# A hybrid mixer and mixture-of-experts layer on one core: read-back, the last block's rows and the final norm arranged otherwise

## What is computed

```python
h = h + moe_ffn(rms_norm(h, norm_ffn_w))       # 4 of 32 experts for each token
out = rms_norm(h, norm_final_w)[:, N_META:]

def run_block(tok, g, e):                      # one block of tokens of one expert
    gu = xt[tok] @ w_gate_up[e] + b_gate_up[e]
    act = glu * sigmoid(1.702 * glu) * (lin + 1.0)
    return (act @ w_down[e] + b_down[e]) * g[:, None]
```

## Time and profile before

| | |
|---|---|
| median of 3 runs | 1552.45 us (1552.38 to 1553.67) |
| the profiled execution | 1552.11 us, span 1550.5 us |
| TensorE busy | 98% of the span |
| VectorE, ScalarE, GpSimd busy | 39%, 16%, 21% |
| mean granted clock of TensorE | 0.993 |
| bytes moved | 476.68 MB, mean 307 GB/s |

### The profile page before, as it was taken

The page is one execution under the profiler, slowest core; times in us unless marked ns, Lnnn a source line. Parts: engine busy times, 40 slices in busy tenths (PEclk is TensorE's granted clock), DMA queues, the critical chain, the costliest instruction groups (busy, mean ns, idle before and its releaser), DMA issues.

```text
span 1550.5 us, 38142 instructions
## 1 busy us (share of the span) xinstructions
PE 1513.8 (98%) x15427; PEld 1005.0 (65%) x15427; DVE 612.0 (39%) x1251; ACT 254.1 (16%) x343; POOL 326.2 (21%) x509
## 2 busy tenths in 40 slices
PE   9999999999999999999999999999999999999996
PEld 7998899877863556555656665655567565565552
DVE  6768988878254132211222112321123211232125
ACT  4533434256130000000000000000000000000011
POOL 1000000000033323322233222332222322233320
PEclk9999999999999999999999999999999999999997
DMA  4222222431368999999999999999999999999937
GB/s 150 83 98 107 89 89 108 162 136 55 136 238 294 416 418 416 406 408 412 410 408 399 400 409 408 403 405 395 414 404 406 403 405 417 410 413 401 368 121 277
DMA packets 80357, 476.68 MB, mean 307 GB/s; under 512 B 17318, under 2 KB 17966, under 8 KB 26434
## 3 DMA queue, kind: packets, MB, share of 16 engines
q1 hardware_dynamic: 66066, 459.14, 73.8%
q0 software_dynamic: 14256, 17.05, 3.1%
HBM read 467.54 MB, written 17.01 MB: 313 GB/s over the span
## 4 chain that ended last, share of the span: by engine, by line
PE 93%; DVE 4%; issue 1%; ACT 1%; DMA 0%; POOLq 0%; DVEq 0%; POOL 0%; ACTq 0%; SPq 0%
PE bank L1768 66%; PE bank L1450 15%; PE bank L1642 6%; PE bank L1469 1%; DVE w_lo L944 1%; PE bank L1578 1%; PE bank L1581 0%; PE bank L1709 0%; PE bank L1593 0%; PE bank L1579 0%; PE bank L1608 0%; DVE reg_tq L1034 0%; PE bank L1837 0%; DVE reg_tq L960 0%; PE bank L1705 0%
## 5 line engine op out<-in xcount | busy, mean ns | idle before, releaser
L1768 PE MATMUL bank<-ring,moe_f 128*32 128x512 f32 (+1 forms) x12216 | 1018.6, 485 | 11.5 <-DVE moe_f L1398 1.1
L1768 PEld LDWEIGHTS bank<-ring,moe_f 128*32 128x32 f32 x12216 | 598.9, 110 | 430.4 <-issue 351.7
L1380 DVE STREAM_TRANSPOSE moe_f<-bank 128x768 f32<-128x768 f32 x32 | 31.5, 983 | 610.2 <-PE bank L1768 610.2
L609 POOL DMA_INDIRECT moe_f<-n_scratch,idx_next x96 | 100.1, 1043 | 438.7 <-DVE moe_f L1364 415.0
L1450 PE MATMUL bank<-n_hi,w_hi 128*128 128x258 f32 (+2 forms) x608 | 190.7, 314 | 1.8 <-DVE w_lo L944 1.8
L1450 PE MATMUL bank<-n_lo,w_hi 128*128 128x258 f32 (+2 forms) x608 | 186.4, 307 | 0.0
L1450 PE MATMUL bank<-n_hi,w_lo 128*128 128x258 f32 (+2 forms) x608 | 186.2, 306 | 0.0
L892 ACT ACTIVATE moe_f<-moe_f 128x768 f32<-128x768 f32 x32 | 27.1, 846 | 717.2 <-DVE moe_f L1384 716.2
L1450 PEld LDWEIGHTS bank<-n_hi,w_hi 128*128 128x128 f32 x608 | 114.4, 188 | 9.7 <-DVE w_lo L944 2.2
L616 POOL DMA_INDIRECT expert_rows<-moe_f,idx_now x96 | 98.3, 1024 | 104.2 <-ACT moe_f L898 82.7
L1450 PEld LDWEIGHTS bank<-n_lo,w_hi 128*128 128x128 f32 x608 | 114.5, 188 | 6.9 <-issue 1.7
(11 more groups left out here) (280 smaller groups left out, 1014.6 us busy)
## 6 DMA issues: line engine op xcount, KB each, us to landing
ring<-in_moe SPq DMA_DIRECT2D x381, 1024.0 KB, 7.9
ring<-in_w_in SPq DMA_DIRECT2D x24, 1024.0 KB, 4.9
ring<-in_w_out SPq DMA_DIRECT2D x8, 1024.0 KB, 4.8
ring<-expert_rows SPq DMA_DIRECT2D x8, 1024.0 KB, 12.2
ring<-acs_scratch SPq DMA_DIRECT2D x4, 1024.0 KB, 7.1
idx_raw<-slot_table POOLq DMA_DIRECT2D x140, 0.8 KB
reg_vcs<-in_xT SPq DMA_DIRECT2D x4, 528.0 KB, 6.1
reg_x<-in_xrow SPq DMA_DIRECT2D x4, 512.0 KB, 4.9
```

What stands on the lines that cost most here:

```text
L609: g.indirect_dma_start(out=xg[:, n, :], out_offset=None, in_=n2_parts, in_offset=bass.IndirectOffsetOnAxis(ap=idx_next[:, 2 * n:2 * n + 1] ...
L1380: v.transpose(glu.rearrange("p b (g r) -> p g b r", g=GRANULES), gate).then_inc(gate_raw, 1)
L1768: ins = mm(out[l * LANE:(l + 1) * LANE, g * width:(g + 1) * width], x[:, at, g * LANE:(g + 1) * LANE], w[:, l * width:(l + 1) * width], st ...
```

## The change

- SyncE waits for the scatters of all blocks but the last before it reads the rows back, and each of the eight loads goes to a ring place of its own among `slot(4)` to `slot(11)`. The count of blocks less one is worked out and stored beside the count.
- The last block's rows are not scattered. `expert_rows` is filled with zeros early on (GpSimd clears `reg_k` and issues eight DMAs of 1 MB between tiles of the mixer), so that its places read as zero. ScalarE and VectorE copy the last block's y out of PSUM to `y_last` [96 slots, 1024], and TensorE adds it to each tile through a matrix `last_of` [96 slots, 512 tokens] that holds the gate where slot and token belong together. VectorE forms `last_of` from the slots' token numbers, from token numbers that GpSimd writes (`tok_iota`), and from a row of the last expert's gates that TensorE spreads over 96 partitions after block 0's down product (four products of 128 columns, from `last_gate`).
- The bias products leave the tail: blocks 2 to 5 are written out on TensorE, and behind each `down(j - 1)` come the two products of one tile, to PSUM banks 3 and 7. VectorE adds them to h2 in the same block.
- In the final norm, the multiply by the reciprocal root and that by the weight are done by GpSimd for tiles 0 to 2, as two instructions. Tile 3 stays with VectorE.

```diff
+        zero_parts = yk_d.rearrange("(n p r) d -> n p (r d)", n=KC, p=P)
...
-        def yk(m):
-            return view(ring, m * TOPK * D, TOPK, D) if m < 3 else view(ring2, 0, TOPK, D)
-
+        def y_of(l, n):
+            at = n * QUARTER
+            return bank[l * LANE:(l + 1) * LANE, 4 + at // 512, at % 512:at % 512 + QUARTER]
+
+        def yk(m, hf):
+            return slot(GU - DN + 2 * m + hf).rearrange("p (k d) -> p k d", k=2)
+
+        y_last = view(moe_f, 3584, D)
+        last_gate = view(late_a, 6336, TT, P)
+        tok_iota = view(late_a, 7456, SEQ)
+        last_of = view(moe_f, 8448, SEQ)
...
-        PART_BANK = [6, 0, 2, 4]
+        PART_BANK = [0, 2, 6, 4]
...
-            hold(y_out, n_blocks * (16 * GRANULES))
+            ahead = sp.value_load(blocks[0:1, 2 * LIST + 5:2 * LIST + 6], min_val=EXPERTS - 1, max_val=LIST - 2)
+            hold(y_out, ahead * (16 * GRANULES))
             for m in range(TT):
                 rows = yk_d.rearrange("(k t) d -> t k d", k=TOPK)[m * P:(m + 1) * P]
                 for hf in range(2):
-                    sp.dma_start(yk(m)[:, 2 * hf:2 * hf + 2, :], rows[:, 2 * hf:2 * hf + 2, :]).then_inc(yk_in[hf][m], 16)
+                    sp.dma_start(yk(m, hf), rows[:, 2 * hf:2 * hf + 2, :]).then_inc(yk_in[hf][m], 16)
             for m in range(TT):
-                sp.wait_ge(o_ready, m + 1)
+                if m < TT - 1:
+                    sp.wait_ge(o_ready, m + 1)
+                else:
+                    sp.wait_ge(o_last, 1)
                 sp.dma_start(out_d[m * P:(m + 1) * P, :], o_sb[m]).then_inc(out_out, 16)
...
+            steps.done(g.memset(reg_k[:, :], 0.0))
...
+            for n in range(KC):
+                pool.wait_ge(xbc_ready, n + 2)
+                pool.dma_start(zero_parts[n], reg_k[:, :]).then_inc(table_filled, 16)
             pool.wait_ge(xbc_ready, XBC_TILES)
+            pool.wait_ge(table_filled, 16 * (1 + KC))
...
+            pool.wait_ge(first_done, 2)
+            for q in range(GRANULES):
+                g.iota(tok_iota[q * LANE:(q + 1) * LANE, :], pattern=[[LANES, SEQ]], base=q, channel_multiplier=0,
+                       allow_small_or_imprecise_dtypes=True).then_inc(slot_iota_ready, 1)
+            pool.wait_ge(slot_iota_ready, 2 + GRANULES)
...
-            hold((y_ready, n_blocks + 1))
-            scatter()
-
+            for m in range(TT - 1):
+                pool.wait_ge(o_scale, m + 1)
+                steps.done(g.tensor_scalar(o_sb[m], o_sb[m], small[:, m:m + 1], None, ALU.mult))
+                steps.settled()
+                g.tensor_tensor(o_sb[m], o_sb[m], w_fin, ALU.mult).then_inc(o_ready, 1)
...
-            evict(n_blocks - 1)
+            act.wait_ge(dn_used, n_blocks * DN + 2 * DN)
+            for l in range(2):
+                for n in range(GRANULES):
+                    ins = a.copy(y_last[n * LANE:(n + 1) * LANE, l * QUARTER:(l + 1) * QUARTER], y_of(l, n))
+            ins.then_inc(y_ready, 1)
...
-            with dve.Fori(1, n_blocks) as j:
-                activations(j, dve.value_load(blocks[0:1, ds(2 * j + 1, 1)], min_val=0, max_val=EXPERTS - 1))
+            last = dve.value_load(blocks[0:1, ds((n_blocks - 1) * 2 + 1, 1)], min_val=0, max_val=EXPERTS - 1)
+            steps.settled()
+            for m in range(TT):
+                v.tensor_scalar(last_gate[:, m, :], ident[:, :], gm[:, m, ds(last, 1)], None, ALU.mult).then_inc(diag_ready, 1)
+
+            def expert_of(j):
+                return dve.value_load(blocks[0:1, ds(2 * j + 1, 1)], min_val=0, max_val=EXPERTS - 1)
+
+            activations(1, 1)
+            with dve.Fori(2, 2 + TT) as j:
+                activations(j, expert_of(j))
+                dve.wait_ge(bias_done, j)
+                row = h2[:, ds(j - 2, 1), :].rearrange("p o (h d) -> p (o h) d", h=2)
+                for hf in range(2):
+                    ins = v.tensor_tensor(row[:, hf, :], row[:, hf, :], bank[:, 3 + 4 * hf, :], ALU.add)
+                ins.then_inc(h2_ready, 1)
+            with dve.Fori(2 + TT, n_blocks) as j:
+                activations(j, expert_of(j))
...
+            dve.wait_ge(idx_moved, n_blocks * 4 + 1)
+            for n in range(GRANULES):
+                p = slice(n * LANE, (n + 1) * LANE)
+                steps.done(v.tensor_copy(pos_f[p, 0:1], idx_now[p, 2 * n:2 * n + 1]))
+            steps.settled()
+            dve.wait_ge(slot_iota_ready, 2 + GRANULES)
+            dve.wait_ge(bias_done, 1)
+            v.scalar_tensor_tensor(last_of[0:BLOCK, :], tok_iota[0:BLOCK, :], pos_f[0:BLOCK, 0:1], bank[0:BLOCK, 6, :],
+                                   ALU.is_equal, ALU.mult).then_inc(diag_ready, 1)
+            dve.wait_ge(dn_used, n_blocks * DN + 2 * DN)
+            for l in range(2, LANES):
+                for n in range(GRANULES):
+                    ins = v.tensor_copy(y_last[n * LANE:(n + 1) * LANE, l * QUARTER:(l + 1) * QUARTER], y_of(l, n))
+            ins.then_inc(diag_ready, 1)
+            dve.wait_ge(h2_ready, 2 * TT)
...
+                if m < TT - 1:
+                    v.reciprocal(small[:, m:m + 1], small[:, m:m + 1]).then_inc(o_scale, 1)
+                    continue
                 steps.done(v.reciprocal(small[:, m:m + 1], small[:, m:m + 1]))
                 steps.settled()
                 v.scalar_tensor_tensor(o_sb[m], o_sb[m], small[:, m:m + 1], w_fin, ALU.mult, ALU.mult
-                                       ).then_inc(o_ready, 1)
+                                       ).then_inc(o_last, 1)
...
-            with pe.Fori(2, n_blocks) as j:
+            pe.wait_ge(diag_ready, TT)
+            for m in range(TT):
+                ins = mm(bank[0:BLOCK, 6, m * P:(m + 1) * P], ones[:, 0:BLOCK], last_gate[:, m, :], start=m == 0, stop=m == TT - 1,
+                         skip_group_check=True)
+            ins.then_inc(bias_done, 1)
+            pe.wait_ge(gmT_ready, 1)
+            pe.wait_ge(bd_in, 16)
+            for j in range(2, 2 + TT):
+                gate_up(j)
+                down(j - 1)
+                pe.wait_ge(h2_ready, j + (TT - 2))
+                for hf in range(2):
+                    ins = mm(bank[:, 3 + 4 * hf, :], gT[0:EXPERTS, j - 2, :], b_down[0:EXPERTS, hf * 512:(hf + 1) * 512], start=True, stop=True)
+                ins.then_inc(bias_done, 1)
+            with pe.Fori(2 + TT, n_blocks) as j:
                 gate_up(j)
                 down(j - 1)
             down(n_blocks - 1, GU)
 
-            pe.wait_ge(gmT_ready, 1)
-            pe.wait_ge(bd_in, 16)
+            pe.wait_ge(diag_ready, 3 * TT + 1)
             for m in range(TT):
-                b = PART_BANK[m]
                 if m == TT - 1:
                     pe.wait_ge(y_ready, n_blocks + 1)
-                for hf in range(2):
-                    mm(bank[:, b + hf, :], gT[0:EXPERTS, m, :], b_down[0:EXPERTS, hf * 512:(hf + 1) * 512],
-                       start=True, stop=False)
-            pe.wait_ge(diag_ready, 2 * TT)
-            for m in range(TT):
+                    pe.wait_ge(diag_ready, 3 * TT + 2)
                 pe.wait_ge(yk_in[0][m], 16)
                 for k in range(2):
                     for hf in range(2):
-                        ins = mm(bank[:, PART_BANK[m] + hf, :], diag[:, 2 * m + k, :], yk(m)[:, k, hf * 512:(hf + 1) * 512],
-                                 start=False, stop=k == 1)
+                        mm(bank[:, PART_BANK[m] + hf, :], diag[:, 2 * m + k, :], yk(m, 0)[:, k, hf * 512:(hf + 1) * 512],
+                           start=k == 0, stop=False)
+                pe.wait_ge(y_ready, n_blocks + 1)
+                pe.wait_ge(diag_ready, 3 * TT + 2)
+                for hf in range(2):
+                    ins = mm(bank[:, PART_BANK[m] + hf, :], last_of[0:BLOCK, m * P:(m + 1) * P], y_last[0:BLOCK, hf * 512:(hf + 1) * 512],
+                             start=False, stop=True)
                 ins.then_inc(part_done, 1)
```

More of the change, by code:

```diff
@@ L311, in build @@
         staged, conv_ready, xbc_ready = sem("staged"), sem("conv_ready"), sem("xbc_ready")
-        dt_done, dt_raw, dt_e = sem("dt_done"), sem("dt_raw"), sem("dt_e")
+        dt_done, dt_e = sem("dt_done"), sem("dt_e")
         acs_ready, wend_e, pk_ready, dtk_done, dtk_ready = (
@@ L332, in build @@
         first_kept, first_turned, stack_ready, xT_half = [sem("first_kept0"), sem("first_kept1")], sem("first_turned"), sem("stack_ready"), sem("xT_half")
[L333 to L334 removed]
+        n2T_done, n2T_ready, logit_done, top_ready, gate_e = (
+            sem("n2T_done"), sem("n2T_ready"), sem("logit_done"), sem("top_ready"), sem("gate_e"))
         rank_done, pos_ready, table_out, list_ready, list_out, list_in = (
@@ L348, in build @@
         diag_ready, part_done = sem("diag_ready"), sem("part_done")
+        o_scale, o_last = sem("o_scale"), sem("o_last")
         sp_passed, pool_passed = sem("sp_passed"), sem("pool_passed")
@@ L1022, in _ @@
```

(7 more changed lines are left out.)

5 lines of the change are left out of this document (1 added, 4 removed).

## The result

The changed kernel took 1557.40 us (median of 7 runs, 1556.43 to 1560.97), the kernel before 1552.45 (7 runs, 1551.75 to 1553.67). The ratio is 1.0033, with a 95% interval of 1.0023 to 1.0043: slower, by more than the 0.2% that can be told. The forecast was 1546.3, its range ended at 1552.5. The profiled execution took 1558.03 us, its span is 1556.4.

The account below looks back on a forecast made before the run. TensorE sets the pace in the experts' blocks, then a chain of waits the tail: 1552.1 - 13.1 + 6.8 + 1.0 - 2.4 - 0.2 + 1.6 + 0.2 = 1546.0, with the median's 0.3 1546.3 us; range 1542.5 to 1552.5.

Parts of the forecast that it names:

- Norm and weight of tiles 0 to 2 on GpSimd: Tail: VectorE's last norm may wait for GpSimd's multiplies, +1.6 us; its gated sums wait 0.1 a tile, +0.2.
- Four blocks written out: Blocks 2 to 5: leaving the loop makes them shorter, like block 1's 31.80 us; -2.4 us (0 to -2.9).
- Bias products: Blocks 2 to 5: eight products of 512 columns on TensorE at 0.855 us each, +6.8 us (6.0 to 10.3).
- The row of gates: After block 0's down product: four TensorE products of 128 columns for the last expert's gates, +1.0 us (0.9 to 1.6).
- Start: Kernel start: GpSimd's extra clearing and the 8 MB of zeros cost 0 (0 to +1.5 us).
- Rows loaded sooner: Tail: the eight 1 MB row loads start before the last block ends and leave the path.
- Last block's y on chip: Tail: scatter, landing and first-load wait give way to PSUM copies; tile 0's add ends at 1515.5, not 1528.64: -13.1 us.
- VectorE sheds the norm: Tail: VectorE loses 1.28 us of work a tile but then waits for ScalarE; three tiles gain only -0.2 us.
- The clock: Blocks 2 to 5: clock falls behind each of four pairs of bias products, 2.6 us each, +10.4: 1556.7; chance 0.08.
- get between the gated sums: Tail: GpSimd's two-input multiply runs between VectorE's two gated sums, delaying the second 1.9 us: 1550.1; chance 0.25.
- No exclusion for two-input forms: Tail: VectorE and GpSimd do not block each other; 1.8 us goes, a late store adds 0.7: 1545.2; chance 0.15.
- the store: Program end: the last 3.1 us of the tail, from the last norm's end to the span's end.

Follow-up runs that it names:

- 128x6 clear: The kernel before with one clear of 128x6 added on GpSimd at the end, waiting for VectorE's last norm: 1554.32 us, ratio 1.0027.
- the folded one: All norms on VectorE and zeros later, plus bias and gate matrix in unused rows of the tail's last-block product, blocks 2 to 31 looped: 1537.32 us, ratio 0.9923.

## Why the prediction was wrong

Against the sum of 1546.0 the profiled execution is 12.0 late: 4.6 up to the last down product, 7.4 behind it.

- **"Norm and weight of tiles 0 to 2 on GpSimd", +1.6 and +0.2: this step failed, and it makes the difference between "no gain" (0.9990 without it) and "slower".** It asked what GpSimd's instructions collide with, not when GpSimd's program ends. The +1.6 did not come: VectorE's last norm ran in 1.29 us from 1544.94, inside GpSimd's one-input multiply of 1544.05 to 1546.88. Instead the end is 10.2 behind the last norm, not 3.1: +7.1. The DRAIN was in the trace of before, 9.9 us long, under a line that no step of mine rested on. I had also given GpSimd 1.0 and 1.9 us for its two forms, from a copy; they take 2.85 and 2.34. The bound of 1.9 for two inputs was too low, and the one-input form lies outside what a copy bounds. Even with my 2.9 a tile, GpSimd ends 3.5 behind tile 3's add and its DRAIN 10.4 behind it, the stores at 6.3 (3.2 + 3.1): +4.1 from the DRAIN alone, close to the 4.5 of the 128x6 clear, where the step had +1.6.
- **"Four blocks written out", -2.4: wrong, 0** (and by its own rows, 4 x 0.58, it was -2.3). The nearest row was block 1's 31.80, taken to be short because it is written out. The kernels without bias products give 129.86 for four written-out blocks and 129.59 for looped ones. The trace says where the short 31.80 comes from: block 1's gate-up took 20.9 us and block 0's down product 10.9, against 20.7 and 11.9 in the loop's first turn (VectorE's transposes at 513.19 and 544.72 mark the ends of gate-up). It is one short down product, and not the code's form: written out, in the kernel without bias products, block 1's down product took 11.7. Why that of block 0 is short stays open.
- **"Bias products", +6.8: right in kind, mis-sized.** 8.1 to 8.3 measured, 2.03 to 2.08 a pair instead of 1.71. The products alone are 1.71; from a pair's start to the next gate-up product it is 1.91 (558.26 to 560.17), and the rest comes around it, at the changeovers. The row of gates gave +0.6 in this execution for my +1.0, and 0.4 to 1.3 in the others. This bullet, the one above and the one below together make the 4.6 us up to the last down product.
- **"Start", 0 (0 to +1.5): +1.2,** inside the bounds. "The DMA engines are mostly idle" held on average, and not at 43 us, where one piece of weights is wanted at once. The zeros three tiles later gave all of it back.
- **"Rows loaded sooner" and "Last block's y on chip", -13.1: right.** Loads went out 6.3 us ahead of the down product's end, as said. The tail of the kernel with all norms on VectorE is 29.0, against 41.5: -12.5, and -12.9 in the folded one. In the changed kernel tile 0's add came 8.06 behind the down product, not 6.5. Of this 1.35 is the first load's landing (7.50 instead of 5.05), and 0.3 TensorE's six products, 5.4 for my 5.1. The copies took longer too (2.6 on VectorE, 2.2 on ScalarE, for 2.1), but the add waited for TensorE. In the folded kernel, without the wait for the load, the add came 6.7 behind.
- **VectorE sheds the norm, -0.2:** right in kind. It waits 1.15 for ScalarE where its norm had been; the steps between adds are 5.16, 5.15 and 5.70, the last longer because a gated sum took 1.84 beside GpSimd's one-input multiply, 0.56 more than without it. The expected 15.6 for three tiles came out at 16.0.
- **The rivals.** The clock stayed at 1.00. GpSimd did not get between the gated sums. "No exclusion for two-input forms" looks nearest for VectorE's last norm, but only because that norm fell beside a one-input multiply: where one fell beside the two-input form it took 1.93 (one and two tiles on GpSimd). The exclusion is there, and the traces show its shape. When GpSimd's two-input multiply starts during a gated sum, it is longer by about what is left of the sum. These are the two sums in the changed kernel, still running for 0.77 and 0.58 us when the multiplies of 1535.36 and 1541.26 start, which take 0.65 and 0.46 more than 2.34:

```profile
1534.85 1.28 DVE L1481 SCALAR_TENSOR_TENSOR reg_x<-ring,gates,reg_x 128x1024 f32<-128x1024 f32 x1
...
1540.56 1.28 DVE L1481 SCALAR_TENSOR_TENSOR reg_x<-ring,gates,reg_x 128x1024 f32<-128x1024 f32 x1
```

When VectorE's instruction starts during a two-input multiply, it ends as if it had been held until 0.2 before the multiply's end (both norms of 1.93). When it starts during a one-input multiply, it ends as if held only until 0.9 after the multiply's start: started 0.34 in, it took 0.56 more; with two tiles on GpSimd 0.69 in, 0.21 more; and the last norm, 0.89 in, took nothing more. The Trainium skill (SBUF — State Buffer, § Who interferes with whom) has the two engines block each other for the whole instruction where VectorE has two SBUF inputs and GpSimd reads SBUF. The rows agree, to 0.1 or 0.2 us, for GpSimd's two-input form; for its one-input form the hold is 0.9 of 2.83 us. The Trainium skill's 4.5 us for 2048 columns (GPSIMD Engine Reference, § Elementwise — side-by-side cycle accounting) gives an estimate of 2.25 for 1024, and the 2.34 measured alone agrees. My 1.9 was worse than that.

My range ended at 1552.5, as each rival moved one term. None touched the last 3.1 us, which I had carried over as "the store".

## What to carry over

- Look at what ends the program on every engine, the closing instructions included, before giving late work to an engine that used to stop early. Here GpSimd needs 7 us from its last instruction to the end; work on it leaves the end alone only if it ends that much ahead of the last store's landing.
- An engine that sets the pace through a long stage is a dear place for work that was hidden before. The eight bias products were free in the old tail and cost 8.1 us in the blocks; in unused rows of a product that was needed anyway they are free again. The kernel that has this, all norms on VectorE and the later zeros is 0.8% faster, where the change as made was 0.3% slower.
- An average DMA share says nothing of the moment in which one piece is awaited; a bulk write can be shifted between such moments.

## What the runs showed of the hardware

- GpSimd's DRAIN ends 6.9 to 7.2 us behind GpSimd's last instruction, be that a scatter, a wide multiply or a clear of 128x6; in the four kernels whose last work on GpSimd was a copy or add of 128x6 long before the end (all norms on VectorE, no bias products, zeros later, bias folded) it is 6.85 us long. VectorE's ends 0.1 us after its last instruction.
- On GpSimd, multiplying 128x1024 float32 by a scalar per partition takes 2.83 to 2.89 us, and by another 128x1024 tile 2.34. A plain copy of 128x2048 took 1.90, so one input does not mean the copy's rate. Beside a VectorE instruction with two SBUF inputs, the one that started second was the one to take longer, by up to 0.65 us on VectorE and 0.85 on GpSimd (a two-input multiply of 3.19); a VectorE instruction that started 0.9 us or more into a one-input multiply lost nothing.
- Two products of 512 columns have records of 1.88 us with 96 rows in use and with 128, and of 1.98 with 32; the next product starts 1.72 after the pair's start in the first two cases and 1.91 in the third. The clock stayed at 1.00 behind those with 32.
- Chips differ by 0.1 us a block: 32.36 between blocks' ends where the kernel before takes 1552.45 or more, 32.27 where it takes 1549.9. That is 2.6 us over 29 blocks, more than some of the terms here, and why ratios on one chip are used. What makes the difference between the chips no run shows.
